# Scale and shift of the first norm as columns, high products of the first tile ahead of its low ones, twelve places for the pieces of w_in

## The reference

```python
mod = einsum('bd,de->be', silu(c), w_ada) + b_ada      # c: one row of 1024 for each sequence; w_ada 1024 x 6144
sh1, sc1, g1, sh2, sc2, g2 = split(mod, 6)
h = layer_norm(x) * (1 + sc1) + sh1
proj = h @ w_in                                        # w_in 1024 x 2048: q, k, v, u
# then rotary, differential attention, Fourier mix, output projection, norm, SwiGLU, norm
```

## Time and profile before

| | us |
|---|---|
| median of three runs | 2984.09 |
| the profiled execution | 2991.88 |
| its span in the trace | 2990.1 |
| TensorE busy in the span | 2848.4 (95%) |
| VectorE | 2289.5 (77%) |
| ScalarE | 1345.3 (45%) |
| GpSimd | 1517.0 (51%) |
| last pass of w_ada ends | 39.86 |
| first product of tile 0 starts | 45.62 |
| turning of q and k of tile 0 starts | 83.39 |

### The profile page before, as it was taken

How to read it: one execution, slowest core, us unless ns; L and a number is a source line. 1 busy time by engine, 2 the same in 40 slices (tenths; PEclk the granted TensorE clock), 3 DMA queues, 4 the chain that set the end, 5 groups by cost and what they waited for, 6 DMA issues and landing times.

```text
span 2990.1 us, 40230 instructions
## 1 busy us (share of the span) xinstructions
PE 2848.4 (95%) x13947; PEld 2392.8 (80%) x13947; DVE 2289.5 (77%) x3092; ACT 1345.3 (45%) x2434; POOL 1517.0 (51%) x1164
## 2 busy tenths in 40 slices
PE   7999998999999998999899999999899999999896
PEld 3888886666666655888799999999899997878784
DVE  5666664988888874556787788898888776588898
ACT  3111112777777774456644343334433443233464
POOL 0233321011111124567767676677776666577786
PEclk9999999999999998999999999999999999999998
DMA  7344347121312104457543454555454367587763
GB/s 263 122 139 125 120 137 181 41 71 57 84 57 71 50 22 170 148 188 231 208 151 116 125 175 166 198 180 180 145 167 162 122 199 268 199 282 273 250 211 113
DMA packets 324773, 460.89 MB, mean 154 GB/s; under 512 B 23318, under 2 KB 207319, under 8 KB 318554
## 3 DMA queue, kind: packets, MB, share of 16 engines
q1 hardware_dynamic: 324572, 458.32, 47.2%
HBM read 308.98 MB, written 149.24 MB: 153 GB/s over the span
## 4 chain that ended last, share of the span: by engine, by line
PE 37%; DVE 10%; DVEq 5%; DMA 4%; POOL 2%; issue 1%; ACT 1%; POOLq 1%; SPq 0%; ACTq 0%
PE tail_bank L2525 6%; PE tail_bank L2526 6%; PE tail_bank L2527 6%; PE tail_bank L2543 4%; PE tail_bank L2545 4%; PE tail_bank L2544 4%; DMA tail_plain<-in_w_dn 3%; DVE tail_plain L2728 2%; PE tail_bank L2463 1%; PE tail_bank L2465 1%; PE tail_bank L2464 1%; POOL tail_rounded L2270 1%; DVE tail_plain L2694 1%; DVEq L2712 1%; DVEq L2700 1%
## 5 line engine op out<-in xcount | busy, mean ns | idle before, releaser
L2270 POOL TENSOR_TENSOR tail_rounded<-tail_plain,tail_rounded 128x512 fp32r<-128x512 f32 x462 | 666.9, 1473 | 287.3 <-ACT tail_rounded L2033 287.2
L2525 PE MATMUL tail_bank<-tail_rounded 128*128 128x384 f32 x1848 | 624.9, 338 | 28.4 <-DVE tail_rounded L2676 18.1
L2527 PE MATMUL tail_bank<-tail_rounded 128*128 128x384 f32 x1848 | 622.1, 337 | 0.0
L2526 PE MATMUL tail_bank<-tail_rounded 128*128 128x384 f32 x1848 | 622.0, 337 | 0.0
L2033 ACT ACTIVATE tail_rounded<-tail_plain 128x512 fp32r<-128x512 f32 x462 | 274.4, 624 | 481.2 <-DVE tail_plain L2662 373.7
L2525 PEld LDWEIGHTS tail_bank<-tail_rounded 128*128 128x128 f32 x1848 | 350.5, 190 | 36.6 <-issue 19.1
L2526 PEld LDWEIGHTS tail_bank<-tail_rounded 128*128 128x128 f32 x1848 | 350.5, 190 | 0.0
L2527 PEld LDWEIGHTS tail_bank<-tail_rounded 128*128 128x128 f32 x1848 | 350.4, 190 | 0.0
L1154 DVE TENSOR_REDUCE att_peak<-att_sc 128x1 f32<-128x1024 f32 x256 | 312.5, 1221 | 42.7 <-PE att_sc L966 36.2
L1058 ACT ACTIVATE att_e<-att_sc,att_peak 128x1024 f32<-128x1024 f32 x256 | 285.4, 1115 | 82.2 <-DVE att_peak L1162 82.2
L965 PE MATMUL att_sc<-held_w_hi 128*128 128x512 f32 x512 | 277.1, 541 | 19.8 <-ACT att_e L1058 14.1
(11 more groups left out here) (298 smaller groups left out, 5492.2 us busy)
## 6 DMA issues: line engine op xcount, KB each, us to landing
tail_plain<-in_w_gu SPq DMA_DIRECT2D x134, 512.0 KB, 5.0
scr_a_d<-tail_plain SPq DMA_DIRECT2D x231, 192.0 KB, 2.1
tail_plain<-scr_a_d SPq DMA_DIRECT2D x85, 256.0 KB, 6.5
scr_out_d<-tail_plain SPq DMA_DIRECT2D x18, 1024.0 KB, 5.0
tail_plain<-scr_out_d SPq DMA_DIRECT2D x18, 1024.0 KB, 7.1
proj_ada<-in_w_ada SPq DMA_DIRECT2D x16, 1024.0 KB, 6.8
held_w_hi<-scr_qs_d SPq DMA_DIRECT2D x128, 128.0 KB, 2.8
scr_h_d<-tail_plain SPq DMA_DIRECT2D x63, 256.0 KB, 4.4
```

The costliest lines, as they stand in the source:

```text
L2270: nc.gpsimd.tensor_tensor(w_lo[:, j, :], operand(F, j), w_hi[:, j, :].bitcast(F32), ALU.subtract).then_inc(wlo_done, 1)
L2525: nc.tensor.matmul(dst, w_hi[:, j, cols], h_hi(b, j)[:, k, :], start=(k == 0), stop=False)
L2526: nc.tensor.matmul(dst, w_hi[:, j, cols], h_lo(b, j)[:, k, :], start=False, stop=False)
L2527: m = nc.tensor.matmul(dst, w_lo[:, j, cols], h_hi(b, j)[:, k, :], start=False, stop=(k == 3))
```

## The change

- The three places of w_ada are taken in another order (`turned`, `u`, `ada`). w_ada is now stationary, in blocks of 128 x 128, and c_silu (128 x 2) moves: for each i 16 products, each begun and closed by itself, into columns of one bank (`by_k`). Nothing is summed on TensorE; `take_cols` reduces over the eight i on VectorE and adds the bias, which arrives as columns with the other biases (six rows of eight instead of four, `gate_rows` and `bias` are larger). `add_bias`, the bias rows, their 16 turns and three semaphores go.
- `transposes(0)` moves from behind i = 4 to behind i = 7; `transposes(1)` stays behind chunk 0 of tile 0; `transposes(2)` moves from ahead of tile 1 to behind its chunk 0, after `turn_qk(0)`.
- The first part of h is two blocks (FIRST = 2) instead of four. In chunk 0 of tile 0 TensorE does the high products of these, waits for their low part, does their low products, and the same for the other six; it waits for the roundings, no longer for GpSimd's part first.
- Pieces: 0 to 7 in four places, then twelve (`turned` 4, `u` 4, `pair` 4). Six are issued between the blocks of w_ada. EARLY = 6 are split before h; ScalarE splits two between the two roundings.
- On VectorE lambda and the bias are taken before piece 5, `norm(1)` after one piece instead of three, `norm(2)` between the rotations of tile 0.

```diff
-        SPLIT_AHEAD, NARROW = 18, 12
+        EARLY, SPLIT_AHEAD, FIRST = 6, 18, 2
...
-            i = n % 4 if n < NARROW else (n - NARROW) % 8
+            i = 8 + n % 4 if n < 8 else (n - 8) % 12
...
             def piece(n):
-                if n >= NARROW + 8:
-                    sp.wait_ge(w_lo_done, n - 7)
-                elif n >= NARROW + 4:
-                    sp.wait_ge(ada_w_used, KD)
+                if n >= 16:
+                    sp.wait_ge(w_lo_done, n - 11)
+                elif n >= 8:
+                    sp.wait_ge(ada_w_used, KD - 1 if n < 12 else KD)
                 elif n >= 4:
                     sp.wait_ge(w_lo_done, n - 3)
...
-                for n in range(pieces, pieces + (0, 0, 1, 2, 2, 2, 2, 1)[i]):
+                for n in range(pieces, pieces + (0, 0, 0, 1, 1, 2, 2, 0)[i]):
...
-                for n in range(NCH):
-                    m = nc.tensor.matmul(acc[0:2, n, :], c_silu[:, i, :], wa[i % RING][:, n // 2, n % 2 * 512:(n % 2 + 1) * 512],
-                                         start=(i == 0), stop=(i == KD - 1))
+                for n in range(2 * KD):
+                    m = nc.tensor.matmul(by_k[:, i, n, :], wa[i % RING][:, n // KD, n % KD * P:(n % KD + 1) * P], c_silu[:, i, :],
+                                         start=True, stop=True)
                 m.then_inc(ada_w_used, 1)
-                if i == 4:
-                    pe.wait_ge(in_landed, 16 * 6)
+                if i == KD - 1:
                     transposes(0)
...
-            pe.wait_ge(rows_done, NCH)
-            for n in range(2 * KD):
-                m = nc.tensor.transpose(cols[:, n, :], rows[:, n * P:(n + 1) * P], keep["ident"][0:2, 0:2])
-            m.then_inc(cols_done, 1)
-            pe.wait_ge(hlo_half, 1)
             for t in range(NT):
-                if 0 < t < NT - 1:
+                if 1 < t < NT - 1:
                     transposes(t + 1)
...
+                    if t == 0 and c == 0:
+                        for ks, hi, lo in ((range(FIRST), hhi_half, hlo_half), (range(FIRST, KD), hhi_done, hlo_done)):
+                            pe.wait_ge(hi, 1)
+                            for k in ks:
+                                pe.wait_ge(w_lo_done, k + 1)
+                                high_products(c, k, t % 2)
+                            pe.wait_ge(lo, 1)
+                            for k in ks:
+                                m = low_product(c, k, t % 2)
...
             def take_cols():
+                mod = keep["mod"][:, 0:2 * KD, :]
+                dve.wait_ge(ada_w_used, KD)
+                nc.vector.tensor_reduce(mod.rearrange("p n r -> p (n r)"), by_k.rearrange("p k n r -> p (n r) k"), AX_X, ALU.add)
+                dve.drain()
+                nc.vector.tensor_tensor(mod, mod, bias[:, 4 * KD:].unsqueeze(2).to_broadcast([P, 2 * KD, 2]), ALU.add)
                 dve.drain()
...
             norm(0)
-            for n in range(3):
+            split_w(0)
+            norm(1)
+            for n in range(1, EARLY - 1):
                 split_w(n)
-            norm(1)
-            for n in range(3, 10):
-                split_w(n)
-            add_bias()
+            take_lambda()
+            take_bias()
+            split_w(EARLY - 1)
             take_cols()
             modulate(0)
-            for n in range(10, SPLIT_AHEAD):
+            for n in range(EARLY, SPLIT_AHEAD):
                 split_w(n)
```

More of the change, by code:

```diff
@@ L140, in project @@
         gate_cols = s.sb("gate_cols", [P, 2, 2, KD])
-        gate_rows = s.sb("gate_rows", [4 * KD, P])
-        bias = s.sb("bias", [P, 4 * KD])
+        gate_rows = s.sb("gate_rows", [6 * KD, P])
+        bias = s.sb("bias", [P, 6 * KD])
         c_in, c_silu = s.sb("c_in", [P, KD, 2]), s.sb("c_silu", [P, KD, 2])
@@ L151, in project @@
         wa = [tile[:].rearrange(form).rearrange("p (h c) -> p h c", h=2) for tile, form in (
-            (ada, "p k c -> p (k c)"), (turned, "p a b c -> p (a b c)"), (u, "p k c -> p (k c)"))]
+            (turned, "p a b c -> p (a b c)"), (u, "p k c -> p (k c)"), (ada, "p k c -> p (k c)"))]
         RING = len(wa)
-        rows = work[0:2].rearrange("r k c -> r (k c)")
         b_rows = gate_rows
@@ L170, in project @@
         h_half, hhi_half, hlo_half = s.sem("h_half"), s.sem("hhi_half"), s.sem("hlo_half")
-        w_landed = [s.sem(f"w_landed{i}") for i in range(8)]
+        w_landed = [s.sem(f"w_landed{i}") for i in range(12)]
         w_hi_done, w_lo_done = s.sem("w_hi_done"), s.sem("w_lo_done")
@@ L288, in _ @@
                     sp.dma_start(x_in[:, i - 2, :], x[ORDER[i - 2]]).then_inc(x_landed[i - 2], 16)
-                if i == 4:
-                    for n, part in enumerate(LATER):
+                if i == 3:
+                    for n, part in enumerate(LATER + (SH1 * D, SC1 * D)):
                         sp.dma_start(b_rows[n * KD:(n + 1) * KD, :],
@@ L448, in transposes, with high_products @@
                 m.then_inc(tp_done, 1)
-            def products(c, k, slot):
+            def high_products(c, k, slot):
                 cols = slice(c * 512, (c + 1) * 512)
@@ L506, in _ @@
                         pe.wait_ge((v_done, u_done)[c - 2], t)
[L507 to L512, removed]
+                    if t == 0 and c == 0:
[7 more added lines that the diff above has]
+                                m = low_product(c, k, t % 2)
+                    else:
+                        for k in range(KD):
+                            if t == 0:
+                                pe.wait_ge(w_lo_done, KD * c + k + 1)
+                            high_products(c, k, t % 2)
+                            m = low_product(c, k, t % 2)
                     m.then_inc(chunk_done[c], 1)
-                    if c == 0 and t == 0:
-                        transposes(1)
                     if c == 0 and t:
                         turn_qk(t - 1)
+                    if c == 0 and t < 2:
+                        transposes(t + 1)
                     if c == 0 and t == NT - 1:
@@ L551, in modulate @@
                                                   keep["mod"][:, k, g:g + 1], ALU.mult, ALU.add)
-                    if t == 0 and k == KD // 2 - 1:
+                    if t == 0 and k == FIRST - 1:
                         ins.then_inc(h_half, 1)
@@ L668, in _ @@
                         split_w(n)
[L669 to L682 removed]
+                    dve.wait_ge(w_lo_done, PIECES)
                 if t and t % 4 == 0:
@@ L689, in _ @@
                     split_qk(t - 1)
+                else:
+                    norm(2)
                 if t == NT - 1:
                     dve.wait_ge(gates_turned, 1)
-                    nc.vector.tensor_copy(gate_rows[:], tp[0:4 * KD, 1, :]).then_inc(gates_out, 1)
+                    nc.vector.tensor_copy(gate_rows[0:4 * KD, :], tp[0:4 * KD, 1, :]).then_inc(gates_out, 1)
                 rotate(t, 1)
```

83 lines of the change are left out of this document (36 added, 47 removed).

## The result

The changed kernel takes 3008.76 us (median of 6 runs, 3004.40 to 3011.73) against 2983.99 beside it (6 runs, 2980.80 to 2989.96): ratio 1.008 [1.007, 1.0091]. It is slower, as forecast, but by 24.8 us and not by 13.7, and it lies above the range. The profiled execution took 3010.01 us, its span is 3008.2. Two runs of the kernel before fell into a slower state of the chip (3900.40 and 7320.35 us) and are left out of every comparison.

A forecast was written before the change was run, and what follows sets the result against it. TensorE, busy 95% of the span, was taken as the bound. With the w_ada stage ending at E = 62.1, E + 35.0 - 83.4 = +13.7 us; 2991.9 + 13.7 = 3005.6, less 7.8, gave 2997.8 us, range 2984 to 3006.

The forecast's parts named there:

- The narrow passes: w_ada stage: 256 two-column passes at half clock, 0.213 us each, so the stage ends at 62.1 us, not 39.86.
- rival 1: w_ada stage: narrow passes at full pace, 27.3 us for 256, transfers bind, 2972 us in all; chance 0.08.
- The chain behind it: From the w_ada stage's end to the first product, through reduction, modulation and rounding: 3.4 us instead of 5.76.
- The first tile: From first product to the turning of q and k, which was to start 35.0 us behind the w_ada stage's end.
- I add 0.3 for this: First tile: 0.3 us allowed for VectorE's pieces, with piece 18 ready just when TensorE wants it.
- 4 us later: First tile: piece 18 is ready 4 us behind tile 1's modulation, two splits taking 3.08 us beside GpSimd's subtraction.
- pieces 6 to 17 are 12 x 0.62: First tile, VectorE: twelve pieces at 0.62 us each, from 4.5 to 12.0 us behind the w_ada stage's end.
- E+35.0: Start of the turning of q and k, 35.0 us behind E, the w_ada stage's end at 62.1 us.
- Rival 4: First tile starves: piece 18 and later ones 2 to 3 us late, clock falls again (2.4), 3002 us; chance 0.07.
- A shift of its start reaches the end of the kernel in full: TensorE's unbroken run of projection products: any delay of its start passes whole to the kernel's end.
- the difference I carry over: Whole kernel: the profiled execution's 7.8 us above the median (2991.9 against 2984.1), taken off the forecast sum.

The follow-up runs named there:

- x_warm_start: Changed kernel plus 8 full products of 512 columns, which nothing reads, ahead of the w_ada stage: 3007.08 us, one run.
- x_warm_mixed: Changed kernel plus 8 full products ahead of the w_ada stage and one behind every third narrow product: 3017.24 us, one run.
- x_columns: Kernel before with one part of the change alone, w_ada stationary with sums and bias as columns: 3011.35 us, ratio 1.008.
- x_moving: Changed kernel with w_ada moving again, sums as rows and 16 turns, all else of the change kept: 2982.09 us, ratio 0.9979.
- x_norm: x_moving with norm(2) put back ahead of the last four pieces: 2983.78 us, one run.
- The delays: Kernel before plus 8, 16, 25, 40 or 60 unread products between w_ada and the turns; ratios 1.0025 (8), 1.006 (25), 1.0099 (40).
- x_keep: x_moving with 24 pieces split ahead instead of 18, plus three unread products ahead of w_ada and three behind the turns: 2976.11 us, ratio 0.9973.

## Why the prediction was right in its mechanism and wrong in its size

*The narrow passes* were right: 0.213 us forecast, 6.81/32 = 0.213 measured; stage's end forecast at 62.1, measured 62.12. x_warm_start and x_warm_mixed show that the clock is the reason (rival 1's price of 0.107 is real, its condition is not met), x_columns and x_moving that this edit alone makes the loss. The Trainium skill's page "TensorE: Matmul & The Clock Gate", section "LDWEIGHTS (loading the stationary operand)", gives 0.107 us for such a load. The spacing of passes agrees with it at full clock (0.10 to 0.11 us) and is twice that at half (0.213).

*The chain behind it* was right: first product forecast 3.4 us behind the stage's end, measured 3.1.

*The first tile* failed in one term. "I add 0.3 for this" was 1.5 us: piece 18's low part was there 20.0 us behind the stage's end, not 18.9, and wanted at 18.6. The prediction had the meeting with GpSimd's subtraction for piece 18 ("4 us later" than the modulation of tile 1, measured 4.1). It lacked the earlier one: "pieces 6 to 17 are 12 x 0.62" has one piece of 2.01 us among them, beside GpSimd's part of 768 columns, and so the modulation of tile 1 began 13.3 us behind the stage's end and not 12.0. I had no wait at the turning itself; it has 0.86 for GpSimd's last step, which comes behind norm(2) now that this stands between VectorE's rotations; in x_norm, which moves norm(2) back, this wait is gone. Forecast E+35.0 with what is owed; measured 98.32 + 0.9 - 62.12 = 37.1. That is 2.1 of the 11.0 us missed. Rival 4 named the place but not the size: no second stretch at half clock came in the tile.

*"A shift of its start reaches the end of the kernel in full"*: +15.8 at the turning became +18.1 in the two spans, 2.3 us more. The delays show the same sign (17.9 for 16.4, 7.5 for 5.2, 29.5 for 26.2), each within its interval of one to one. What these 2 us are was not settled. Most of it came in attention (16.1, then 18.8), a stage that took 641.5 to 644.8 us over the 18 traces; and before's own mark moved by 4.1 us from trace to trace, so a difference of 2 between single traces may be chance.

*The step that failed* is "the difference I carry over": 7.8 us, by which the profiled execution of before lay above its median. Profile against profile the forecast was +13.7 and the measured +18.1. So 7.8 - 1.25 = 6.5 us of the miss come from taking 7.8 off where after's profiled execution lay only 1.25 us above its median. What the 7.8 was: before's profile had the second fall of the clock, some 5 us, and the rest is spread of other stages; after's two profiled executions have the fall too, and lie only 1.25 and 1.38 us above their medians. The likely account is that the fall is in the median run of after and not in that of before, so that subtracting it took away a cost that stays in the changed kernel. The terms of 2.1, 2.3 and 6.5 us make up the 11.0 (10.9 by rounding). That the median of before lacks the fall and that of after has it is inferred: only profiled executions show the clock in this stretch. Two things on record fit it. The 68 runs of before fall into 47 up to 2986.64 us and 21 from 2988.12 on; the trace with the fall took 2991.88, the two without it 2981.38 and 2986.23. And of the twelve timed runs of after, the three with a mean granted clock of 0.982 took 3001.9 to 3005.5 us, the six at 0.980 or less, both profiled ones among them, 3007.3 to 3011.7. Whether and why the changed kernel has it more often stays open; the delays exclude that lateness alone brings it. The Trainium skill's page "TensorE: Matmul & The Clock Gate", Part 1, says that the chip judges the engine's activity in windows that run on whatever the kernel does, so that one kernel meets them at another phase each time; a fall that is there in one profile of before and not in two others fits that, and no run here shows the windows.

## What to carry to other kernels

Before turning a product round so that the wide matrix is stationary and a column or two move, price it at half clock: a stage that was weight loads and narrow passes alone let the granted clock go, even at 100% busy (x_warm_start), and never got it when it began at half. When a profiled execution lies far from the median of its kernel, find out what makes the difference before carrying it over, and take two more profiles of the kernel before, since a stretch at half clock that comes and goes can be as large as a small effect (5 us here, where x_moving's gain is 2 to 7). Waits of an in-order chain move on when one is removed: price the next one, on GpSimd too. Take the instructions of a row apart before using its mean: 3.06 us for two was 2.46 and 0.68.

## What the runs showed of the hardware that was not expected

- The same instructions of the same kernel can meet a fall of the granted clock in one execution and not in the next: the 68 runs of before went from 2980.16 to 2994.25 us, and a trace with the fall behind attention takes some 5 us more in that stretch (310.6 against 305.8 in the mean).
- A subtraction of 128x512 on VectorE that began while GpSimd's subtraction was running ended 0.55 us behind GpSimd's, in all 37 cases of 18 traces, and so took 1.34 to 2.48 us; all others took 0.67 to 0.69.
- The granted clock fell from 1.00 to 0.50 some 5.3 us behind the end of the last full product (10.4, then 15.7) while TensorE was 100% busy with passes of two columns (x_warm_start), and held with a product of 512 columns behind every six such passes (x_warm_mixed).
- With three products that nothing reads in idle time ahead of it, the first block of w_ada took 3.61 us (x_keep); without them it took 5.00 to 6.51.
